# Hybrid decoder step on one core: weights of two experts asked for earlier, and gathered rows transposed by VectorE instead of TensorE

## The chip, the core and the metric

The kernel runs on one core of a Trainium2 chip. A core has five engines that run their own instruction streams and meet at semaphores: TensorE (PE, matrix products and transposes into PSUM), VectorE (DVE), ScalarE (ACT), GpSimd (POOL) and SyncE (SP). SP and POOL also ask for the transfers between HBM and SBUF, which 16 DMA engines carry out. The metric is the device time of one execution in microseconds; less is better.

## The reference, cut to what matters

One layer: a token mixer (mLSTM and retention heads, one input and one output projection) and then a mixture of experts. 512 prompt rows and 64 sample rows, 576 rows of 1024 values in float32. What the change touches is the mixture:

```
def moe(h, w_router, b_router, we_g, we_u, we_d, ws_g, ws_u, ws_d):
    s = sigmoid(h @ w_router)                       # 64 experts
    eidx = ...                                      # 8 experts for each row, from 4 of 8 groups
    wts = s at eidx, normalised, times 2.5
    for each block of 128 rows of one expert e (tok, wt):
        xb = h[tok]
        hb = silu(xb @ we_g[e]) * (xb @ we_u[e])    # 1024 -> 256
        acc[tok] += wt * (hb @ we_d[e])             # 256 -> 1024
    return acc + (silu(h @ ws_g) * (h @ ws_u)) @ ws_d
```

An expert has 2 MB of gate and up weights and 1 MB of down weights: 64 experts, some 200 MB, each read once.

## The kernel before

Every engine's program is written out by hand, and every wait in it is a semaphore wait that holds up all that stands behind it on that engine. The first part (about 450 us) is the mixer. Then come `y_mm` (the output projection, row tile by row tile), the second norm, the router and the shared expert's up products, and then the expert stage.

**Blocks.** The experts are sorted by how many rows chose them (the first three, `NPRE`, are experts 0, 1, 2, whatever their counts, so that their weights can be asked for before the ids are known). `CAPS` gives each a fixed number of 32-row pieces, 192 in all, so 48 blocks (`NBK`) of 4 pieces, numbered 0 to 47. A block can hold pieces of up to four experts.

**A block on each engine.** `place` (DVE, L2202 and L2205) builds a 0/1 matrix for the block three ahead, `find_idx` (PE, L1536) turns it into row numbers, `idx_out` (DVE, L2241 to L2243) stores them. POOL gathers the rows (`gather`, L790) into one of three buffers `xg`, three blocks ahead. `x_T` (PE, L1549) transposes the 128 x 1024 rows by eight 128 x 128 transposes into two PSUM banks, and ScalarE (`xT_evac`, L1053) and VectorE (`xT_evac`, L2247) copy half each into `xT`. `up` (PE, L1561) multiplies by the gate and up weights, in 8 chunks of the contraction. `silu` (ACT) and `gated` (DVE, L2255) follow, `hh_T` (PE, L1572) transposes the 256 columns, `down` (PE, L1584) multiplies by the down weights, two copies (`out_rows`, DVE L2262) bring the rows to `yo`, and POOL scatters them (`scatter`, L806).

The order on PE in block b is `up(b)`, `hh_T(b-1)`, `x_T(b+1)`, `find_idx(b+3)`, `down(b-1)`. In the last block, 47, `hh_T` stands between the first six chunks of `up` and the last two. The order on DVE is `place(b+3)`, `xT_evac(b+1)`, `gated(b)`, `idx_out(b+3)`, `out_rows(b-1)`.

**Weights.** Five slots (`WSLOTS`) hold the weights of five experts; the r-th expert in the sorted order uses slot r % 5. SP asks for the weights in a fixed order: the gate and up weights (`load_gate_up`, L616) of expert r once `up` of the last block of expert r-5 is done, the down weights (`load_dn`, L620) once its `down` is. One slot lies in `x_sb` and `hT`, where the residual rows and the router's input are until late. Two slots lie at the start of `mem`, where the mixer's output weights and temporaries are, one behind them, and one (`NM`) in a stretch that holds small tables and the last retention state. SP's order before the stage: `b_router`, the stores of the five tiles of `mixed_rows`, the shared expert's down weights, then (when the rows for the gathers are stored) experts 0 and 1, the gate and up weights of expert 2, and, when the sorted ids are there (`tab_ready`), the gate and up weights of experts 3 and 4; the down weights of experts 2, 3 and 4 come when the shared up products are done.

Of the kernel before, what the change touches and what calls it, by code (L numbers as in the profile page):

```python
# [14 lines left out]
P = 128  # L15
# [31 lines left out]
XSLOT = 2  # L47
XSLOT2 = 4
OVSLOTS = [0, 1, 3]
XG = 3  # L50
OVMAX = 4 * U
# [83 lines left out]
def build(nc, A, O, K):  # L135

    ctx = ExitStack()
    with ctx:
# [151 lines left out]
        def yT(h):  # L290
# [14 lines left out]
        W_AT = [0, WSZ, None, w2_at, NM]  # L305
# [4 lines left out]
        at = w2_at + WSZ  # L310
        hhT, at = carve(mem, at, [FJ * BLK])
# [9 lines left out]
        dn4, e_ = carve(mem, e_, [FJ, D])  # L321
        at = max(at + NT * D, e_)
# [47 lines left out]
            P_ready idx_mm idx_ready gat0 gat1 gat2 xgT_t xgT_a xgT_d eup egs ehh ehT_t ehT edn eout_a eout_d sct0 sct1  # L370
# [92 lines left out]
        def wview(r):  # L463

            if slot(r) == XSLOT:
                return x_flat[:, 0:2 * KC * FE].rearrange("p (c n) -> p c n", c=KC), dnX
            at_ = W_AT[slot(r)]
            gu = mem[:, at_:at_ + 2 * KC * FE].rearrange("p (c n) -> p c n", c=KC)
            if slot(r) == XSLOT2:
# [4 lines left out]
        GU_LOADED = [("ld_gu0", 0), ("ld_gu1", 0), ("ld_gu2", 0), ("ld_gu3", 0), ("ld_a1", 32)]  # L474
        DN_LOADED = [("ld_d0", 0), ("ld_d1", 0), ("ld_d2", 0), ("ld_d3", 0), ("ld_a2", 32)]
# [54 lines left out]
        def _(sp):  # L530
# [115 lines left out]
            sp.wait_ge(S["xgT_t"], NBK)  # L646
# [12 lines left out]
            def last_rows():  # L659
                sp.wait_ge(S["xgT_a"], nov + (NBK + 1))  # L660
                sp.wait_ge(S["xgT_d"], nov + (NBK + 1))
# [5 lines left out]
            sp.wait_ge(S["xgT_a"], NBK)  # L667
            sp.wait_ge(S["xgT_d"], NBK)
# [43 lines left out]
        def _(pool):  # L712
# [80 lines left out]
            def ahead(n, q, g):  # L793
                pool.wait_ge(S["idx_ready"], n + 1)
                if not isinstance(n, int):
                    pool.wait_ge(S["xgT_t"], n - 1)
# [48 lines left out]
        def _(act):  # L845
# [227 lines left out]
            def body(n, j, s, i):  # L1073
                silu(n, j)
                xT_evac(n + 1, j + 1)
# [18 lines left out]
            overflow(act, nov, body, lambda: xT_evac(NBK, NBK))  # L1094
# [16 lines left out]
        def _(pe):  # L1111
# [427 lines left out]
            def x_T(n, j, s=None):  # L1539

                g = gbuf(n, j)
                pe.wait_ge(S[f"gat{g}"], gcount(n, j, s))
                if not (isinstance(n, int) and n == 0):
                    pe.wait_ge(S["xgT_a"], n)
                    pe.wait_ge(S["xgT_d"], n)
# [6 lines left out]
            def up(n, j, parts, cs=range(KC)):  # L1552

                pe.wait_ge(S["xgT_a"], n + 1)
                pe.wait_ge(S["xgT_d"], n + 1)
# [42 lines left out]
            def body(n, j, s, i):  # L1598
# [3 lines left out]
                x_T(n + 1, j + 1, s + 1)  # L1602
# [14 lines left out]
            x_T(0, 0)  # L1617
# [27 lines left out]
            def first_blocks():  # L1645
                whole = [(slice(0, BLK), 0, None)]
                find_idx(NBK, NBK, whole)
                x_T(NBK, 0, 0)
                find_idx(NBK + 1, NBK + 1, whole)

            def last_done():
                pe.wait_ge(S["xgT_a"], nov + (NBK + 1))
                pe.wait_ge(S["xgT_d"], nov + (NBK + 1))
# [8 lines left out]
            for name in ("xgT_a", "xgT_d", "ehh", "ehT", "eout_a", "eout_d", "idx_ready"):  # L1662
                pe.wait_ge(S[name], NBK)

            def shared_down(o, js=range(FJ)):
                t, kp = COMBINE[o]
                n = ROWS[t]
                if o == 0:
                    pe.wait_ge(S["ld_br"], 32)
# [38 lines left out]
        def _(dve):  # L1708
# [370 lines left out]
            dve.wait_ge(S["ld_br"], 32)  # L2079
# [165 lines left out]
            def xT_evac(n, j):  # L2245
                dve.wait_ge(S["xgT_t"], n + 1)
                cp(xT[:, j % 2, 4 * BLK:8 * BLK], ps[1][:, :]).then_inc(S["xgT_d"], 1)  # L2247
# [16 lines left out]
            def body(n, j, s, i):  # L2264
                place_more(n + 2, j + 2, s + 2)
                gated(n, j)
                xT_evac(n + 1, j + 1)
# [31 lines left out]
            def first_blocks():  # L2299
# [3 lines left out]
                xT_evac(NBK, NBK)  # L2303
# [184 lines left out]
```

## Time and profile before

| | |
|---|---|
| median of 3 runs | 1125.05 us (1124.58 to 1125.45) |
| the profiled execution's own time | 1126.64 us |
| its span (first to last instruction) | 1124.8 us |
| TensorE busy | 1094.1 us, 97% of the span |
| VectorE busy | 462.7 us, 41% |
| ScalarE busy | 236.4 us, 21% |
| mean over the span that the DMA moved | 300 GB/s |

The profile lists each engine's instructions with start and duration, in microseconds from the start of the span, and the packets of the DMA. An "idle" time of an instruction is how long its engine stood still ahead of it, with the instruction or the transfer that ended the wait. "To landing" is the time from the issue of a transfer until its last piece is there. L numbers are lines of the kernel.

### The profile page before, as it was taken

Reading aid. Unit: us, or ns where it says so; the run is one execution under the profiler, and the core shown is the slowest. Engines: PE = TensorE matmul, PEld = TensorE weight load, DVE = VectorE, ACT = ScalarE, POOL = GpSimd, SP = SyncE. Lnnn points to the kernel's source line nnn. Section 1 sums busy time; section 2 is a strip of 40 time slices with the busy share of each in tenths; the row PEclk is TensorE's granted clock in tenths of the full one; section 3 lists DMA queues with packets and bytes.
Section 4 is the critical chain, followed back from the end, with each engine's and each line's share of the span. In section 5 each row is a group of like instructions: output and inputs, shape, how many; then the busy total and the mean of one; then the engine's idle time right before and its main releaser. Section 6 shows DMA issues by size and latency. Waiting matters only on the chain.

```text
span 1124.8 us, 16922 instructions
## 1 busy us (share of the span) xinstructions
PE 1094.1 (97%) x6443; PEld 575.1 (51%) x6443; DVE 462.7 (41%) x1286; ACT 236.4 (21%) x516; POOL 135.3 (12%) x163
## 2 busy tenths in 40 slices
PE   6999999999999999999999999999999999999896
PEld 3456677777877545754343443443444444343232
DVE  2218541565456645843274233233232232331157
ACT  4131241222133123211111111111111111111111
POOL 0210000000020010121112112111111121121100
PEclk9999999999999999999999999999999999999999
DMA  9857622021170273899999999999999999999598
GB/s 370 326 207 295 227 79 75 1 85 51 62 266 7 103 255 120 311 365 426 423 425 426 424 417 425 425 416 396 421 409 384 426 399 400 417 391 370 209 412 344
DMA packets 51655, 337.16 MB, mean 300 GB/s; under 512 B 9637, under 2 KB 14089, under 8 KB 30831
## 3 DMA queue, kind: packets, MB, share of 16 engines
q1 hardware_dynamic: 33710, 287.32, 63.0%
q0 software_dynamic: 17856, 48.68, 11.8%
q8 instruction: 54, 0.88, 0.3%
q14 instruction: 35, 0.28, 0.1%
HBM read 311.30 MB, written 37.24 MB: 310 GB/s over the span
## 4 chain that ended last, share of the span: by engine, by line
PE 91%; DMA 4%; DVE 2%; ACT 1%; issue 1%; SPq 0%; DVEq 0%; POOLq 0%; ACTq 0%
PE bank L1561 30%; PE bank L1584 15%; PE bank L1257 10%; PE bank L1276 5%; PE bank L1549 4%; DMA mem<-expert_out_rows 3%; PE bank L1375 3%; PE bank L1376 3%; PE bank L1170 3%; PE bank L1493 3%; PE bank L1254 3%; PE bank L1145 1%; PE bank L1572 1%; PE bank L1340 1%; PE bank L1154 1%; PE bank L1128 1%
## 5 line engine op out<-in xcount | busy, mean ns | idle before, releaser
L1561 PE MATMUL bank<-mem 128*32 128x512 f32 (+2 forms) x1488 | 304.5, 594 | 0.6 <-DVE mem L2247 0.6
L1561 PEld LDWEIGHTS bank<-mem 128*32 128x32 f32 (+2 forms) x1488 | 100.6, 126 | 166.0 <-issue 166.0
L1584 PE MATMUL bank<-mem 128*32 128x512 f32 (+2 forms) x744 | 157.0, 596 | 0.1
L2247 DVE COPY mem<-bank 128x512 f32<-128x512 f32 x48 | 33.2, 691 | 283.3 <-PE bank L1549 283.3
L1257 PE MATMUL bank<-hT,mem 128*128 128x288 f32 x512 | 133.3, 410 | 1.0 <-ACT mem L935 1.0
L1257 PEld LDWEIGHTS bank<-hT,mem 128*128 128x128 f32 x512 | 93.9, 190 | 25.7 <-issue 2.4
L1561 PE MATMUL bank<-x_sb,mem 128*32 128x512 f32 (+2 forms) x416 | 99.3, 594 | 0.0
L1065 ACT ACTIVATE mem<-bank 128x256 f32<-128x256 f32 x48 | 18.4, 384 | 313.0 <-PE bank L1572 312.8
L1584 PEld LDWEIGHTS bank<-mem 128*32 128x32 f32 (+2 forms) x744 | 48.7, 126 | 61.4 <-issue 60.6
L2262 DVE COPY hT<-bank 128x512 f32<-128x512 f32 x48 | 33.2, 691 | 85.7 <-PE bank L1584 85.6
L790 POOL DMA_INDIRECT mem<-ffn_in_rows,idxg x32 | 32.9, 1028 | 264.5 <-DVE idxs L2243 211.0
L806 POOL DMA_INDIRECT expert_out_rows<-hT,idxs x48 | 48.7, 1015 | 114.8 <-DVE hT L2262 110.4
L1071 ACT ACTIVATE hT<-bank 128x512 f32<-128x512 f32 x48 | 28.7, 597 | 140.8 <-PE bank L1584 140.8
L1561 PEld LDWEIGHTS bank<-x_sb,mem 128*32 128x32 f32 (+2 forms) x416 | 32.2, 127 | 49.4 <-issue 49.4
L1276 PE MATMUL bank<-mem 128*128 128x512 f32 x128 | 56.3, 594 | 0.0
L1584 PE MATMUL bank<-hT,mem 128*32 128x512 f32 (+2 forms) x208 | 51.0, 596 | 1.1 <-ACT mem L1065 1.1
L2205 DVE SCALAR_TENSOR_TENSOR mem<-mem,c_full 128x160 bf16<-128x160 f32 (+3 forms) x77 | 43.9, 570 | 0.3 <-issue 0.3
L1375 PE MATMUL bank<-hT,mem 128*128 128x288 f32 x128 | 42.4, 413 | 0.0
L1376 PE MATMUL bank<-hT,mem 128*128 128x288 f32 x128 | 41.5, 406 | 0.0
L1276 PEld LDWEIGHTS bank<-mem 128*128 128x128 f32 x128 | 23.8, 190 | 27.4 <-issue 27.2
L1053 ACT ACTIVATE mem<-bank 128x512 f32<-128x512 f32 x48 | 28.7, 597 | 38.8 <-PE bank L1549 38.8
L2255 DVE SCALAR_TENSOR_TENSOR mem<-mem,wtab,bank 128x128 f32<-128x128 f32 x96 | 29.1, 344 | 17.3 <-ACT mem L1059 17.3
(400 smaller groups left out, 1281.2 us busy)
## 6 DMA issues: line engine op xcount, KB each, us to landing
mem<-k_w_exp SPq DMA_DIRECT2D x51, 2048.0 KB, 23.3
mem<-in_w_exp_down SPq DMA_DIRECT2D x51, 1024.0 KB, 22.7
x_sb<-k_w_exp SPq DMA_DIRECT2D x13, 2048.0 KB, 21.4
mem<-k_w_ada SPq DMA_DIRECT2D x8, 2048.0 KB, 9.0
mem<-k_w_in SPq DMA_DIRECT2D x7, 2048.0 KB, 9.7
hT<-in_w_exp_down SPq DMA_DIRECT2D x13, 1024.0 KB, 25.4
mem<-expert_out_rows SPq DMA_DIRECT2D x6, 2048.0 KB, 16.5
mem<-k_w_head SPq DMA_DIRECT2D x4, 2048.0 KB, 18.4
```

What stands on the lines that cost most here:

```text
L806: pool.indirect_dma_start(y_d[:, :], bass.IndirectOffsetOnAxis(idxs[:, q:q + 1], 0), yo[:, q % 2, :], None, bounds_check=T * TOPK - 1, oob ...
L1170: i = mm(ps[t][:, :], hT[:, k, t * P:(t + 1) * P], ring[:, 0, k * 512:(k + 1) * 512], start=k == 0, stop=k == KC - 1)
L1254: i = mm(bank[0:n, 0:2 * DH], hT[:, k, c * P:c * P + n], w[:, k, 2 * DH * hf:2 * DH * (hf + 1)], start=k == 0, stop=k == KC - 1)
L1257: i = mm(bank[:, 0:TH], w[:, k, c * P:(c + 1) * P], hT[:, k, hf * TH:(hf + 1) * TH], start=k == 0, stop=k == KC - 1)
L1276: i = mm(y_half(t, hf), yT(k)[:, t * P:t * P + n], wo[:, k, hf * 512:(hf + 1) * 512], start=k == 0, stop=k == 2 * H - 1)
L1375: mm(A0[:, 0:TH], st, hT[:, k, 0:TH], start=k == 0, stop=k == KC - 1)
L1376: i = mm(A1[:, 0:TH], st, hT[:, k, TH:T], start=k == 0, stop=k == KC - 1)
L1493: i = mm(ps[bu if m else bg][:, 0:TH], gu_s[:, m, k, j * P:(j + 1) * P], hT[:, k, hf * TH:(hf + 1) * TH], start=k == 0, stop=k == KC - 1)
L1549: i = tr(ps[c // 4][:, (c % 4) * BLK:(c % 4 + 1) * BLK], xg[g][:, c * P:(c + 1) * P], ident[:, :])
L1561: i = mm(bank[sl, :], xT[:, j % 2, c * BLK + sl.start:c * BLK + sl.stop], wview(r)[0][:, c, :], start=c == 0, stop=c == KC - 1)
L1584: i = mm(ps[4 + hf][sl, :], hhT[:, k * BLK + sl.start:k * BLK + sl.stop], wview(r)[1][:, k, hf * 512:(hf + 1) * 512], start=k == 0, stop=k ...
L2205: return stt(pm, p.to_broadcast([P, NT, w]), off, iota[:, 0:w].unsqueeze(1).to_broadcast([P, NT, w]), ALU.add, ALU.is_equal)
```

## The change

Two edits.

1. The slots are numbered anew: the first is the one at `NM`, with its down weights where the mixer's gates were, then the two at the start of `mem`, the one behind them, and last the one in `x_sb` and `hT`. Expert 0 is asked for right behind `b_router`, expert 1 when `y_mm` is done (in front of the store of the fifth tile of `mixed_rows`), expert 2 with its down weights when the rows for the gathers are stored. The shared expert's down weights follow behind it, and `b_router` gets another semaphore.
2. For the blocks from number 10 on (`TURNED`), VectorE transposes the gathered rows from `xg` to `xT` by itself: `turn`, 16 instructions of 32 partitions x 256 values, each of eight 32 x 32 blocks. `x_T` and its two copies remain for blocks 0 to 9. From block 9 on, `hh_T` stands between the first six chunks of `up` and the last two. The semaphores `xgT_t` and `xgT_d` for the finished rows give way to `xT_ready`.

```
@@ constants @@
-XSLOT = 2
-XSLOT2 = 4
-OVSLOTS = [0, 1, 3]
+EXTSLOT = 0
+XSLOT = 4
+OVSLOTS = [1, 2, 3]
 XG = 3
+TURNED = 10
...
-        W_AT = [0, WSZ, None, w2_at, NM]
+        W_AT = [NM, 0, WSZ, w2_at, None]
...
+        at += gate_at - at
+        dn4, at = carve(mem, at, [FJ, D])
...
@@ SP @@
-            sp.dma_start(brow, A["b_router"][0].partition_broadcast(P)).then_inc(S["ld_br"], 16)
-            for t in range(NT):
-                sp.wait_ge(S["x1_done"], t + 1)
-                sp.dma_start(x1_d[t * P:t * P + ROWS[t], :], x_sb[0:ROWS[t], t, :]).then_inc(S["st_x"], 16)
-            load_down(sp, dn_s, A["w_sh_down"][0], S["ld_br"])
-            sp.wait_ge(S["h2T_t"], NT)
-            sp.wait_ge(S["h2_st0"], 16 * ((NT + 1) // 2))
-            sp.wait_ge(S["h2_st1"], 16 * (NT // 2))
+            sp.dma_start(brow, A["b_router"][0].partition_broadcast(P)).then_inc(S["ld_col"], 16)
...
-            for r in range(2):
-                load_gate_up(r, r)
-                load_dn(r, r)
+            load_gate_up(0, 0)
+            load_dn(0, 0)
+            for t in range(NT):
+                if t == NCH:
+                    sp.wait_ge(S["y_mm"], NT)
+                    load_gate_up(1, 1)
+                    load_dn(1, 1)
+                sp.wait_ge(S["x1_done"], t + 1)
+                sp.dma_start(x1_d[t * P:t * P + ROWS[t], :], x_sb[0:ROWS[t], t, :]).then_inc(S["st_x"], 16)
+            sp.wait_ge(S["h2T_t"], NT)
+            sp.wait_ge(S["h2_st0"], 16 * ((NT + 1) // 2))
+            sp.wait_ge(S["h2_st1"], 16 * (NT // 2))
+            load_gate_up(2, 2)
+            load_dn(2, 2)
+            load_down(sp, dn_s, A["w_sh_down"][0], S["ld_br"])
             sp.wait_ge(S["st_x"], 16 * NT)
-            load_gate_up(XSLOT, XSLOT)
             sp.wait_ge(S["tab_ready"], 1)
...
             load_gate_up(NPRE, id3)
-            load_gate_up(NPRE + 1, id4)
+            load_gate_up(XSLOT, id4)
             sp.wait_ge(S["gu_mm"], NSH)
-            load_dn(XSLOT, XSLOT)
             load_dn(NPRE, id3)
-            load_dn(NPRE + 1, id4)
+            load_dn(XSLOT, id4)
...
             sp.wait_ge(S["eup"], max(LASTB[r] for r in range(NE) if slot(r) == XSLOT) + 1)
-            sp.wait_ge(S["xgT_t"], NBK)
+            sp.wait_ge(S["xT_ready"], NBK)
...
@@ POOL, ahead() @@
                 elif n >= XG:
-                    pool.wait_ge(S["xgT_t"], n - XG + 1)
+                    pool.wait_ge(S["xT_ready"], n - XG + 1)
...
@@ ACT @@
-                if b < NBK - 1:
+                if b + 1 < TURNED:
                     xT_evac(b + 1, b + 1)
...
@@ PE @@
             for b in range(NBK):
                 new_gu(b)
-                if b < NBK - 1:
-                    up(b, b, pieces(b))
-                else:
-                    up(b, b, pieces(b), range(KC - 2))
+                split = KC if b + 1 < TURNED else KC - 2
+                up(b, b, pieces(b), range(split))
...
                     hh_T(b - 1)
-                if b == NBK - 1:
-                    up(b, b, pieces(b), range(KC - 2, KC))
-                if b < NBK - 1:
-                    x_T(b + 1, b + 1)
+                if split < KC:
+                    up(b, b, pieces(b), range(split, KC))
+                if b + 1 < TURNED:
+                    x_T(b + 1)
...
@@ DVE @@
+            def turn(n, j, s=None):
+
+                g = gbuf(n, j)
+                dve.wait_ge(S[f"gat{g}"], gcount(n, j, s))
+                dve.wait_ge(S["eup"], n - 1)
+                rows = xg[g].rearrange("s (c d) -> s c d", c=KC)
+                cols = xT[:, j % 2, :].rearrange("d (c s) -> d c s", c=KC)
+                for q in range(P // QS):
+                    for a in range(P // QS):
+                        sl, dl = slice(q * QS, (q + 1) * QS), slice(a * QS, (a + 1) * QS)
+                        i = dve.transpose(cols[dl, :, sl], rows[sl, :, dl])
+                i.then_inc(S["xT_ready"], 1)
...
-                if b < NBK - 1:
+                if b + 1 < TURNED:
                     xT_evac(b + 1, b + 1)
+                elif b + 1 < NBK:
+                    turn(b + 1, b + 1)
                 gated(b, b)
```

## Rows read from the trace of the kernel before

**Rows 1.** The page: busy time of the engines, and the DMA in 40 slices.
```profile
PE 1094.1 (97%) x6443; PEld 575.1 (51%) x6443; DVE 462.7 (41%) x1286; ACT 236.4 (21%) x516; POOL 135.3 (12%) x163
...
DMA  9857622021170273899999999999999999999598
```

**Rows 2.** Waits of TensorE, 485 to 1058 us: total, times, longest.
```profile
PE bank L1584 <- ACT mem L1065: 1.1, 1, 1.1
PE bank L1561 <- DVE mem L2247: 0.6, 1, 0.6
```

**Rows 3.** TensorE in order of time, block 20 and the start of 21.
```profile
723.34 7.13 PE L1561 MATMUL bank<-x_sb,mem 128*128 128x512 f32 x16
730.31 0.38 PE L1572 MATMUL bank<-c_ident,mem 128*128 128x128 f32 x2
730.53 1.04 PE L1549 MATMUL bank<-c_ident,mem 128*128 128x128 f32 x8
731.49 0.29 PE L1536 MATMUL bank<-mem 128*32 128x7 bf16 x20
731.75 3.67 PE L1584 MATMUL bank<-mem 128*128 128x512 f32 x8
735.35 1.06 PE L1561 MATMUL bank<-mem 128*32 128x512 f32 x8
```

**Rows 4.** Stretches: busy PE, PEld, DVE, ACT, POOL; clock, DMA share, GB/s.
```profile
485.00:765.00 280.00, 279.18 (x2080) 117.87 (x2082) 100.94 (x267) 42.64 (x92) 47.24 (x47) 1.00 1.01 420
765.00:1045.00 280.00, 280.00 (x1783) 116.23 (x1775) 79.72 (x227) 43.87 (x95) 45.29 (x45) 1.00 0.98 399
1010.00:1020.00 10.00, 10.00 (x57) 4.28 (x54) 3.22 (x11) 1.37 (x4) 1.00 (x1) 1.00 0.76 291
```

**Rows 5.** Gate/up loads (L616) issued 706 to 708 us: issue, landing.
```profile
L616 SPq DMA_DIRECT2D mem<-k_w_exp x2: 333/333/333, 706.7 to 707.8; - x2
...
DMA to landing us min/median/max: 28.0/30.4/32.9
```

**Rows 6.** The same, issued 1028 to 1030 us.
```profile
L616 SPq DMA_DIRECT2D mem<-k_w_exp x1: 333/333/333, 1028.8 to 1028.8; - x1
...
DMA to landing us min/median/max: 15.0/15.0/15.0
```

**Rows 7.** TensorE in order of time, block 47: start of `up`, start of `down`.
```profile
1045.06 0.64 PE L1561 MATMUL bank<-x_sb,mem 128*64 128x512 f32 x1
...
1052.50 1.89 PE L1584 MATMUL bank<-mem 128*64 128x512 f32 x8
```

**Rows 8.** Gate/up load issued 1004 to 1006 us: issue, landing.
```profile
L616 SPq DMA_DIRECT2D mem<-k_w_exp x1: 333/333/333, 1004.7 to 1004.7; - x1
...
DMA to landing us min/median/max: 18.5/18.5/18.5
```

**Rows 9.** SP's queue in order of time, 395 to 520 us.
```profile
460.07 0.33 SPq L616 DMA_DIRECT2D mem<-k_w_exp  x1
...
485.14 0.89 SPq L616 DMA_DIRECT2D mem<-k_w_exp  x2
487.25 0.34 SPq L620 DMA_DIRECT2D hT<-in_w_exp_down  x1
```

**Rows 10.** VectorE's groups by shape, 600 to 1000 us: busy us, mean ns.
```profile
L2247 DVE COPY mem<-bank 128x512 f32<-128x512 f32 x34 | 23.5, 691 | 209.3 <-PE bank L1549 209.3
...
L2205 DVE SCALAR_TENSOR_TENSOR mem<-mem,c_full 128x480 bf16<-128x480 f32 x16 | 10.4, 653 | 0.0
...
L2205 DVE SCALAR_TENSOR_TENSOR mem<-mem,c_full 128x160 bf16<-128x160 f32 x16 | 5.1, 321 | 0.0
```

**Rows 11.** The gathers (L790), all 48.
```profile
DMA to landing us min/median/max: 4.6/10.6/12.3
```

**Rows 12.** Stretches behind the last block, columns as in rows 4.
```profile
1061.00:1064.00 3.00, 0.20 (x2) 0.00 (x0) 0.69 (x1) 0.60 (x1) 0.96 (x1) 1.00 0.30 93
1064.00:1068.00 4.00, 3.92 (x6) 1.16 (x7) 0.22 (x1) 0.00 (x0) 0.00 (x0) 0.57 0.24 79
```

More of the change, by code:

```diff
@@ L320, in build @@
         bcG, e_ = carve(mem, e_, [2, D])
-        dn4, e_ = carve(mem, e_, [FJ, D])
-        at = max(at + NT * D, e_)
+        at = e_
         R, at = carve(mem, at, [8, NT, NE], dt=BF16)
@@ L468, in wview @@
             gu = mem[:, at_:at_ + 2 * KC * FE].rearrange("p (c n) -> p c n", c=KC)
-            if slot(r) == XSLOT2:
+            if slot(r) == EXTSLOT:
                 return gu, dn4
@@ L472, in wview @@
             return gu, dn
-        GU_LOADED = [("ld_gu0", 0), ("ld_gu1", 0), ("ld_gu2", 0), ("ld_gu3", 0), ("ld_a1", 32)]
-        DN_LOADED = [("ld_d0", 0), ("ld_d1", 0), ("ld_d2", 0), ("ld_d3", 0), ("ld_a2", 32)]
+        GU_LOADED = [("ld_a1", 32), ("ld_gu0", 0), ("ld_gu1", 0), ("ld_gu2", 0), ("ld_gu3", 0)]
+        DN_LOADED = [("ld_a2", 32), ("ld_d0", 0), ("ld_d1", 0), ("ld_d2", 0), ("ld_d3", 0)]
         def gu_sem(r):
@@ L659, in last_rows @@
             def last_rows():
-                sp.wait_ge(S["xgT_a"], nov + (NBK + 1))
-                sp.wait_ge(S["xgT_d"], nov + (NBK + 1))
+                sp.wait_ge(S["xT_ready"], nov + (NBK + 1))
                 sp.wait_ge(S["sct0"], 16 * (NBK // 2) + 16 * ((nov + 1) // 2))
@@ L666, in _ @@
             overflow(sp, nov, body, last=last_rows)
-            sp.wait_ge(S["xgT_a"], NBK)
-            sp.wait_ge(S["xgT_d"], NBK)
+            sp.wait_ge(S["xT_ready"], NBK)
             for k in range(2):
@@ L795, in ahead @@
                 if not isinstance(n, int):
-                    pool.wait_ge(S["xgT_t"], n - 1)
+                    pool.wait_ge(S["xT_ready"], n - 1)
                 elif n >= XG:
-                    pool.wait_ge(S["xgT_t"], n - XG + 1)
+                    pool.wait_ge(S["xT_ready"], n - XG + 1)
                 pool.sem_inc(S["pool_step"], 1)
@@ L1093, in _ @@
             out_rows(NBK - 1, NBK - 1)
-            overflow(act, nov, body, lambda: xT_evac(NBK, NBK))
+            overflow(act, nov, body)
             for i, (t, _) in enumerate(COMBINE):
@@ L1537, in find_idx, with x_T @@
                 i.then_inc(S["idx_mm"], 1)
[L1539 to L1543, printed above, removed]
+            def x_T(n):
+                g = gbuf(n, n)
+                pe.wait_ge(S[f"gat{g}"], gcount(n, n))
+                if n:
                     pe.wait_ge(S["xgT_a"], n)
-                    pe.wait_ge(S["xgT_d"], n)
+                    pe.wait_ge(S["xT_ready"], n)
                 else:
@@ L1552, in up @@
             def up(n, j, parts, cs=range(KC)):
-                pe.wait_ge(S["xgT_a"], n + 1)
-                pe.wait_ge(S["xgT_d"], n + 1)
+                if isinstance(n, int) and n < TURNED:
+                    pe.wait_ge(S["xgT_a"], n + 1)
+                pe.wait_ge(S["xT_ready"], n + 1)
                 if not (isinstance(n, int) and n < 2):
@@ L1601, in body @@
                 up(n, j, whole)
-                x_T(n + 1, j + 1, s + 1)
                 find_idx(n + 2, j + 2, whole)
@@ L1616, in _ @@
             shared_up(KC // 2)
-            x_T(0, 0)
+            x_T(0)
             shared_up(2)
@@ L1647, in first_blocks @@
                 find_idx(NBK, NBK, whole)
-                x_T(NBK, 0, 0)
                 find_idx(NBK + 1, NBK + 1, whole)
             def last_done():
-                pe.wait_ge(S["xgT_a"], nov + (NBK + 1))
-                pe.wait_ge(S["xgT_d"], nov + (NBK + 1))
+                pe.wait_ge(S["xT_ready"], nov + (NBK + 1))
                 pe.wait_ge(S["ehh"], nov + NBK)
@@ L1661, in _ @@
             overflow(pe, nov, body, first_blocks, last_done)
-            for name in ("xgT_a", "xgT_d", "ehh", "ehT", "eout_a", "eout_d", "idx_ready"):
+            for name in ("xT_ready", "ehh", "ehT", "eout_a", "eout_d", "idx_ready"):
                 pe.wait_ge(S[name], NBK)
@@ L1668, in shared_down @@
                 if o == 0:
-                    pe.wait_ge(S["ld_br"], 32)
+                    pe.wait_ge(S["ld_br"], 16)
                     pe.wait_ge(S["sh_ready"], NSH)
@@ L2077, in _ @@
                     bcB[0:n, 1, :].rearrange("p (q c) -> p q c", c=KC), ALU.add).then_inc(S["h2_ready"], 1)
-            dve.wait_ge(S["ld_br"], 32)
+            dve.wait_ge(S["ld_col"], 32)
             dve.memset(gs12, -MARK)
@@ L2246, in xT_evac @@
                 dve.wait_ge(S["xgT_t"], n + 1)
[L2247 removed]
+                cp(xT[:, j % 2, 4 * BLK:8 * BLK], ps[1][:, :]).then_inc(S["xT_ready"], 1)
+            def turn(n, j, s=None):
[9 more added lines that the diff above has]
+                i.then_inc(S["xT_ready"], 1)
             def gated(n, j):
@@ L2266, in body @@
                 gated(n, j)
-                xT_evac(n + 1, j + 1)
+                turn(n + 1, j + 1, s + 1)
                 idx_out(n + 2, j + 2, s + 2)
@@ L2302, in first_blocks @@
                 place_more(NBK + 1, NBK + 1, 1)
-                xT_evac(NBK, NBK)
+                turn(NBK, 0, 0)
                 idx_out(NBK + 1, NBK + 1)
```

3 lines of the change are left out of this document (1 added, 2 removed).

## The prediction

> **What bounds the kernel now.** I read the page first, then the waits of TensorE, then one block of the expert stage in order of time, then the DMA side of that stage. The page shows TensorE busy for 1094.1 of 1124.8 us and, from the eighteenth of its 40 slices on, the DMA engines at 9 tenths almost throughout [rows 1]. Two things are full at once, so the question is which of them would give way. From 485 to 1058 us TensorE waited twice, 1.7 us in all [rows 2]. It is the engine that sets the pace. A block takes 12.0 us: from the start of `up` of one block at 723.34 to the start of the next at 735.35 [rows 3]. The eight transposes of the gathered rows (`x_T`, L1549) start at 730.53, and the work behind them at 731.49: 0.96 us of the block.
>
> Now the transfers. Over the first 280 us of the stage the engines moved 420 GB/s at a mean share of 1.01, over the next 280 us 399 GB/s at 0.98 [rows 4]. A 2 MB gate/up load would need 5 us at 420 GB/s. The pair issued at 706.7 and 707.8 took 28.0 and 32.9 us [rows 5]: each stands behind several others, and the queue of loads is never empty there. Next, how early a load is. By the list of capacities the load issued at 706.7 is that of the thirtieth expert, which block 21 needs first, and block 21 starts at 735.35 [rows 3]. It lands at 706.7 + 28.0 = 734.7. That is 0.65 us before use. The last load of all is issued at 1028.8, lands 15.0 us later at 1043.8 [rows 6], and block 47 starts at 1045.06 [rows 7]: 1.26 us early. So loads are just in time twice, at the middle and at the very end, with the queue full. TensorE sets the pace, with the DMA about one microsecond behind it.
>
> One more row says how hard this second limit is. The load issued at 1004.7 took 18.5 us and landed at 1023.2 [rows 8], yet from 1010 to 1020 us the mean share of the 16 engines was 0.76 [rows 4]. Some engines had run dry while others still held pieces of a load that nobody could use before the last piece. The mean share understates how busy the last engine is.
>
> **The change part by part.** *Transposes off TensorE.* For blocks 10 to 47 the eight transposes go, 38 times. The order inside these blocks becomes six chunks of `up`, `hh_T`, two chunks of `up`, `find_idx`, `down`. Block 47 has this order already, without `find_idx`: from the start of `up` to the start of `down` it takes 1052.50 - 1045.06 = 7.44 us [rows 7]. An ordinary block takes 731.75 - 723.34 = 8.41 us, of which `find_idx` holds 0.26 us [rows 3]. TensorE saves 8.41 - 7.44 - 0.26 = 0.71 us a block, 27.0 us in all, if it waits for nothing else.
>
> *What the transfers let through.* Nothing of the 64 loads, gathers and scatters goes away. A load is still issued when a block frees its slot; issued earlier, it stands longer in the same queue. The time at which the last gate/up load lands moves only by what is taken off the queue ahead of it.
>
> *The early loads.* Before, experts 0, 1 and 2 are asked for from 460.07 on, and what needs the sorted ids follows at 485.14; the third expert's down weights wait until 487.25, in the midst of the full stretch [rows 9]. After, expert 0 is asked for right behind `b_router`, before the first row store, expert 1 in front of the last store of `mixed_rows`, and expert 2 takes their old place together with its down weights. For experts 0 and 1 this gains nothing by itself: they were in time already. What gets out of the queue behind 485 is that one 1 MB transfer: 1.05 MB / 420 GB/s = 2.5 us. Experts 3 and 4 still wait for the ids. The cost of the early loads: the fifth store of `mixed_rows` stands behind 3 MB, 7.5 us at 420 GB/s, and with it the clearing of the third gather buffer. Cover is the stretch from 460.07 to 485.14 [rows 9], so I take nothing; without the cover it would be 7.5 us. `w_sh_down` moves behind expert 2, and is now wanted only after the last block. The read back of `mixed_rows` into `x_sb` waits for block 45 instead of 47, since the slot there is now another one: it stands behind the last weights on SP's queue, so no load waits for it, and its 2.36 MB, 5.6 us at 420 GB/s, are through before the last scatter.
>
> *VectorE.* Per block it drops one copy of 0.69 us and gets 16 transposes of 32 x 256 values. The trace has no transpose on VectorE. The fixed part and the slope come from two forms of the same line: 160 columns take 0.321 us, 480 take 0.653 [rows 10], so 1.04 ns a column and 0.155 us fixed, 0.42 us for 256. Bounds: 0.32 (the 160-column form) and 0.69 (the copy of 512 columns). I take 0.42, since these forms go column by column, and a transpose moves each value once, too: 16 x 0.42 = 6.7 us. VectorE was busy 79.72 us of 280 [rows 4], 3.4 us of a block of 12.0. Afterwards: 3.4 - 0.69 + 6.7 = 9.4 us. That fits into a block, and TensorE waits for none of it. On VectorE the `gated` product and the index row stand behind the turn; both are wanted in the next block, `gated` only after six chunks of `up`. The gather, asked for at the end of a block's chain, landed after 12.3 us at worst [rows 11]; the turn that needs it comes two blocks later, so it is in time by a few tenths or more. ScalarE loses a copy, and nothing waited 1 us or more for that one [rows 2].
>
> The Trainium skill speaks against this part: in "VectorE: DVE Perf Modes", section "The three transpose paths", VectorE does 32 x 32 blocks only, and the rules for authors send a full 128 x 128 transpose to TensorE. Its 311 ns for 128 x 128 values of bf16 would make an estimated 2.5 us for eight, instead of my 6.7; the time that I forecast is the same by either, as both are covered.
>
> *The sum.* After the early blocks TensorE runs ahead of the loads and waits for them. Block 47 can start when the last gate/up load lands: 1043.8 - 2.5 = 1041.3 instead of 1045.06, so 3.7 us. A cost comes back: where TensorE stood still for 2.8 of 3 us, the clock granted in the next 4 us was 0.57, a mean of the full 2.4 GHz and the lower level of 1.2 GHz [rows 12]. If a wait ahead of block 47 does that, it costs 4 x (1 - 0.57) = 1.7 us. Bounds 0 and 1.7; I take 0.7, since most such waits fall where the loads are late anyway. 3.7 - 0.7 = 3.0 us. What follows block 47 is unchanged. The profiled execution took 1126.64 us for a span of 1124.8, and the median is 1125.05, so taking 3.0 us from the median gives 1122.0 us.
>
> **The rivals.** *A, the idle share of the DMA is usable.* If 399 GB/s in the second half were no limit but only a lack of requests, earlier requests would fill it: 280 x (1 - 399/420) = 14 us more, 1108 us. For it: the 0.76 between 1010 and 1020. Against it: a load was outstanding all that time. The Trainium skill, "DMA: Bandwidth & Descriptors", section "iDMA fabric", has it that a bulk load runs at the pace of its slowest engine; by that A is out, and the trace agrees with its 18.5 us beside a share of 0.76.
>
> *B, the loads are hidden anyway.* Then all 27.0 us come off: 1098 us. Against it: 0.65 us at block 21, and 1.26 us at block 47.
>
> *C, slower: VectorE becomes the bound.* The place is the turn, in front of `gated` on one engine. The point is (12.0 - 2.7) / 16 = 0.58 us for a transpose. At 0.69 us, the row of the 512-column copy, a block takes 2.7 + 11.0 = 13.7 us, 1.7 us more, 38 times: 1125 + 65 = 1190 us. At 0.60 it is 1136 us. For it: no transpose has been seen. Against it: 256 columns are half of that copy's.
>
> *D, nothing changes.* The queue is so full that the 2.5 us and the last 1.3 us are lost to scatters which, with TensorE ahead, come in front of the last loads, and to the clock: between 1123.5 and 1127 us.
>
> **How the numbers follow.** About 0.2%, 2.25 us, is what a measurement of this kernel can tell from no change. My forecast, 1119 to 1123.5 us, gets 0.55; A, with what lies between it and the forecast, 0.15; B 0.03; C, or another late step of VectorE, 0.12; D 0.15. The likeliest case gives 1122.0. For 8 in 10 the range reaches to A, 1108, and up through D to the mildest form of C, 1130. Faster: most of the forecast (0.41 of 0.55, since its upper end is at the limit), A and B: 0.59. Same: the rest of the forecast and most of D: 0.26. Slower: C and a little of D: 0.15.
>
> **What would show it.** L1549 stands in the profile 80 times instead of 384. TensorE, which waited 1.7 us, waits some 20 to 27 us for the weights in the blocks from about the eighteenth on, and the blocks without a wait take 11.2 to 11.3 us. The shares of the DMA rise a little, and the last gate/up load lands at about 1041 us, not some 15 us earlier. VectorE's transposes take about 0.42 us and its busy share rises to 0.8 of a block. I am wrong if TensorE waits little and the span falls by over 8 us (then the DMA had room), or if TensorE waits for VectorE instead of the loads (then C).

## The result, and the profile after

The changed kernel takes 1128.67 us (median of 6 runs, 1127.59 to 1130.65), the kernel before 1125.25 us beside it: a ratio of 1.0029, 95% interval 1.0018 to 1.004. It is slower by 0.3%. The forecast was 1122.0 us and faster; the time lies inside the range of 1108 to 1130.

The profiled execution took 1129.68 us, 3.04 us more than the one of before. The page, the lines that answer to [rows 1], and VectorE's transposes:

```profile
PE 1070.1 (95%) x6139; PEld 541.8 (48%) x6139; DVE 698.8 (62%) x1856; ACT 218.1 (19%) x478; POOL 135.5 (12%) x163
...
PEclk9999999999999999999999999999999899899999
DMA  9857622022170386699999999999999999999598
...
L2257 DVE STREAM_TRANSPOSE mem<-mem 32x256 f32<-32x256 f32 x400 | 174.2, 435 | 5.3
...
L2257 DVE STREAM_TRANSPOSE mem<-x_sb 32x256 f32<-32x256 f32 x208 | 90.6, 436 | 2.7
```

TensorE works 24 us less, a transpose takes 0.436 us, and VectorE has 570 instructions more. The waits of TensorE from 485 to 1070 us (total, times, longest), to be read against [rows 2], and the stretches with the columns of [rows 4]:

```profile
PE bank L1564 <- issue: 23.1, 8, 6.0
PE bank L1587 <- DMA mem<-in_w_exp_down: 1.9, 1, 1.9
...
PE bank L1564 <- DMA mem<-k_w_exp: 0.7, 1, 0.7
```

```profile
485.00:765.00 280.00, 270.48 (x1974) 106.62 (x1976) 192.79 (x490) 36.21 (x79) 47.03 (x46) 0.99 1.01 418
765.00:1045.00 280.00, 265.16 (x1581) 93.78 (x1573) 224.01 (x576) 32.39 (x71) 45.21 (x45) 0.98 0.98 397
...
1048.00:1052.00 4.00, 4.00 (x14) 1.42 (x12) 0.00 (x0) 0.00 (x0) 0.00 (x0) 0.57 0.98 368
```

TensorE's 24 us come back as 25.7 us in which it stands still for weights. Most of it is put down to "issue", that is, to nothing that the profile names. `up` waits for several semaphores at once; at block 47 the wait ends 0.1 us behind the last part of the load (1047.14 and 1047.23 us), and I read the others in the same way. The DMA moves no more than before. Block 47, TensorE in order of time, against [rows 7], and the last gate/up load, against [rows 6]:

```profile
1047.23 7.07 PE L1564 MATMUL bank<-mem 128*64 128x512 f32 x24 [3.07 <-issue]
1054.22 0.44 PE L1575 MATMUL bank<-c_ident,mem 128*128 128x128 f32 x2
```

```profile
L611 SPq DMA_DIRECT2D mem<-k_w_exp x1: 332/332/332, 1027.5 to 1027.5; - x1
...
DMA to landing us min/median/max: 19.6/19.6/19.6
```

For the sum at the end, where the first six chunks of block 47 end in the kernel before, and the last scatter before and after:

```profile
1050.36 0.44 PE L1572 MATMUL bank<-c_ident,mem 128*128 128x128 f32 x2
...
1062.78 4.95 DMA expert_out_rows<-hT,idxs
```

```profile
1066.64 3.23 DMA expert_out_rows<-hT,idxs
```

The load is asked for 1.3 us earlier than before and lands 3.3 us later, at 1047.1 instead of 1043.9. Block 47 waits for it and starts 2.17 us later. Its first six chunks take 6.99 us (1047.23 to 1054.22); before, they took 5.30 (1045.06 to 1050.36). In the changed kernel TensorE had stood still for 3.07 us, and the granted clock from 1048 to 1052 us is 0.57. That makes 3.9 us. The chain of waits behind it gives 0.8 us back. The last scatter takes 1.7 us less (3.23 us, not 4.95; the read back of `x_sb` is now asked for at 1044.79 instead of 1052.71, but no run shows that this is the reason), and the last read of the experts' rows takes 1.4 us more. At the end 3.1 us are left.

### The profile page after: what moved, and what is told of

It reads as the page before. It is cut to its first block, busy times and chain, and to the rows that moved or that the text cites. A ratio compares the mean times of both kernels' runs of the same rounds, so it can differ in the third digit from the quotient of the medians.

```text
span 1127.9 us, 16862 instructions
## 1 busy us (share of the span) xinstructions
PE 1070.1 (95%) x6139; PEld 541.8 (48%) x6139; DVE 698.8 (62%) x1856; ACT 218.1 (19%) x478; POOL 135.5 (12%) x163
## 4 chain that ended last, share of the span: by engine, by line
PE 84%; DMA 10%; issue 2%; DVE 2%; ACT 1%; SPq 0%; DVEq 0%; POOLq 0%; ACTq 0%
PE bank L1564 27%; PE bank L1587 14%; PE bank L1259 10%; PE bank L1278 5%; DMA mem<-expert_out_rows 3%; DMA mem<-in_w_exp_down 3%; PE bank L1377 3%; PE bank L1378 3%; PE bank L1495 3%; PE bank L1172 3%; PE bank L1256 3%; DMA mem<-k_w_exp 2%; PE bank L1147 1%; PE bank L1575 1%; PE bank L1342 1%
## 5 line engine op out<-in xcount | busy, mean ns | idle before, releaser
L1564 PE MATMUL bank<-mem 128*32 128x512 f32 (+2 forms) x1504 | 331.9, 607 | 24.4 <-issue 23.1
L1564 PEld LDWEIGHTS bank<-mem 128*32 128x32 f32 (+2 forms) x1504 | 106.6, 129 | 206.6 <-issue 205.0
L2257 DVE STREAM_TRANSPOSE mem<-mem 32x256 f32<-32x256 f32 x400 | 174.2, 435 | 5.3
L1587 PE MATMUL bank<-mem 128*32 128x512 f32 (+2 forms) x752 | 166.1, 604 | 1.1 <-ACT mem L1068 1.1
L1564 PE MATMUL bank<-x_sb,mem 128*32 128x512 f32 (+2 forms) x400 | 109.9, 607 | 0.0
L2257 DVE STREAM_TRANSPOSE mem<-x_sb 32x256 f32<-32x256 f32 x208 | 90.6, 436 | 2.7
L1587 PEld LDWEIGHTS bank<-mem 128*32 128x32 f32 (+2 forms) x752 | 52.4, 128 | 72.2 <-issue 71.4
L1587 PE MATMUL bank<-hT,mem 128*32 128x512 f32 (+2 forms) x200 | 56.4, 605 | 1.9 <-DMA mem<-in_w_exp_down 1.9
```

The lines of the kernel that those rows point to most:

```text
L1564: i = mm(bank[sl, :], xT[:, j % 2, c * BLK + sl.start:c * BLK + sl.stop], wview(r)[0][:, c, :], start=c == 0, stop=c == KC - 1)
L1587: i = mm(ps[4 + hf][sl, :], hhT[:, k * BLK + sl.start:k * BLK + sl.stop], wview(r)[1][:, k, hf * 512:(hf + 1) * 512], start=k == 0, stop=k ...
L2257: i = dve.transpose(cols[dl, :, sl], rows[sl, :, dl])
```

## The experiments

All numbers are medians of 4 to 11 runs; the kernel before had 1125.0 to 1126.1 us beside them. "Parts": the trace has the 16 times at which each load raises its semaphore. There are 16 DMA engines, and I read each time as the landing of one engine's share; the trace doesn't say which engine's. Sorted, in us from the start of the span, for the last gate/up load of the kernels that matter:

```
                              asked for  1st     8th     12th    15th    16th part (us)
before                        1028.8   1036.7  1037.3  1038.2  1043.7  1043.9
changed                       1027.5   1036.0  1036.8  1037.4  1042.0  1047.1
one transpose (e3)            1021.2   1029.9  1030.5  1036.3  1041.9  1042.1
early loads alone (e1)        1028.1   1036.1  1036.6  1037.3  1040.2  1040.9
early loads, dummy work (e16) 1027.8   1037.2  1037.6  1038.8  1041.2  1044.8
both transpose (e4)           1034.9   1043.1  1043.7  1044.1  1044.4  1047.2
before, dealt by eights (e9)  1033.0   1041.2  1042.7  1050.2  1053.7  1053.9
before, even (e13)            1028.5   1036.6  1037.0  1037.2  1037.3  1038.4
changed, even (e10)           1011.0   1019.9  1021.6  1022.9  1024.0  1030.8
even, one transpose (e14)     1008.3   1017.7  1023.3  1024.4  1025.0  1027.1
even, 16 small (e17)          1013.3   1022.2  1022.6  1023.4  1025.3  1031.8
even, one large (e18)         1008.1   1017.1  1023.5  1024.2  1025.1  1026.8
even, reversed (e19)          1019.1   1027.8  1028.9  1034.1  1037.0  1037.3
```

### Which half does it, and by way of which engine

e1, the early loads alone, is `TURNED = 48`. e2, the turn alone, has the old slots and the old order on SP. In e3 the loop of `turn` is one instruction, `dve.transpose(cols[0:QS, :, 0:QS], rows[0:QS, :, 0:QS])`. e4 adds this where `x_T` stood:

```
+                elif b + 1 < NBK:
+                    for c in range(KC):
+                        tr(ps[c // 4][:, (c % 4) * BLK:(c % 4 + 1) * BLK], ident[:, :], ident[:, :])
```

> The early loads and the new slots alone: TensorE transposes the gathered rows of all 48 blocks, VectorE turns none. Theory 1 (VectorE's 16 transposes a block slow the transfers of the slowest DMA engine) and theory 2 (TensorE running ahead harms itself: earlier scatters in front of the last loads, half clock behind each wait) both expect 1122 to 1125.3 us: loads land some 2.5 us earlier than before at block 21, TensorE waits for none, and the read back of x_sb, asked for two blocks earlier, may give up to 2 us at the end. Theory 3 (the early loads themselves do the harm) expects over 1126 us.

> The turn by VectorE from block 10 on alone: slots, their semaphores and SyncE's order of loads as before. Theories 1 and 2 expect the changed kernel's time and the 2.5 us that the early loads took off the queue: 1130 to 1132 us, with more waits of TensorE for weights from about block 18 on. Theory 3 expects less than the changed kernel, under 1127 us.

> The changed kernel with 1 of the 16 transposes in each turn, so that most of the columns that up reads are not the gathered rows; TensorE's order is that of the changed kernel. Theory 1 (VectorE's traffic slows the transfers) expects the last gate/up load at about 1041.5 us and a time of 1121 to 1124 us. Theory 2 (TensorE ahead of the loads) expects the time of the changed kernel, 1127.5 to 1130 us, and the same windows of half clock.

> The changed kernel, and TensorE does eight transposes of a constant in each block from the tenth on, where x_T stood, into banks that nobody reads: TensorE keeps the pace of before, VectorE does all of its transposes. Theory 1 expects loads as late as in the changed kernel, with waits of TensorE of some us near the end, 1126 to 1129 us. Theory 2 expects no waits, no half clock, and 1122 to 1125.3 us as for the early loads alone.

Measured: e1 1125.18 us (ratio 0.9994, 0.9985 to 1.0003), e2 1131.23 (1.004, 1.0027 to 1.0053), e3 1122.02 (0.9962, 0.9948 to 0.9975), e4 1132.41 (1.0055, 1.0041 to 1.0068). The early loads do no harm, and no good while TensorE sets the pace, so theory 3 falls. The 2.5 us that were counted for them fit the landings of the last load, which is 2.1 us earlier with the turn (1047.1 us, in e2 1049.3) and 2.9 us earlier without it (1040.9, before 1043.9). In the times they are not shown clearly: the medians of e2 and the changed kernel are 2.6 us apart, their ratios only 1.2 us, and the intervals of the ratios overlap. In e3 TensorE runs ahead and waits much as in the changed kernel, and the time is the forecast's. Its waits for the loads, and its block 47:

```profile
PE bank L1564 <- issue: 17.7, 7, 4.7
...
1042.23 5.37 PE L1564 MATMUL bank<-mem 128*64 128x512 f32 x24 [0.72 <-issue]
```

So theory 2 falls: what costs 6.7 us is VectorE's 15 further transposes. e4 missed both expectations: the dummy transposes took 1.07 us a block, block 47 started at 1051.26 us, TensorE waited for no weight, and its own longer blocks set the time. Its parts tell something all the same: 15 of them land within 1.3 us, and the last one 2.8 us behind those, though TensorE doesn't run ahead. Such a late part comes with the turn, then, and not with TensorE's pace.

### Traffic, waiting, or something else

e5 has, in place of 15 transposes, 13 copies of 32 x 256 values within PSUM, each waiting for the one before. In e6 each `dve.transpose(a, b)` of the turn is a plain copy. The turn of e11 has its first 13 transposes where the turn stood, and the last 3 behind the index row:

```
                 elif b + 1 < NBK:
-                    turn(b + 1, b + 1)
+                    turn(b + 1, b + 1, part=range(13))
                 gated(b, b)
                 if b + XG < NBK:
                     idx_out(b + XG, b + XG)
+                if TURNED <= b + 1 < NBK:
+                    turn(b + 1, b + 1, part=range(13, 16))
```

> The changed kernel with 1 of the 16 transposes in each turn and, ahead of it, 13 copies one after the other of 32 x 256 values from one PSUM bank into another: VectorE is held about as long as by 16 transposes (so the index row and the next gather are asked for as late), but SBUF is hardly read or written for it. Theory 1a (VectorE's traffic in SBUF slows the transfers) expects the time with one transpose, 1121 to 1124 us. Theory 1b (the turn holds VectorE, and what stands behind it is asked for later) expects that of the changed kernel, 1127.5 to 1130 us.

> The changed kernel with each of the 16 transposes replaced by a copy of the same 32 x 256 values between the same places, so that nothing is transposed inside a 32 x 32 square. If any traffic of VectorE between these places slows the transfers, the time stays at 1127 to 1130 us; if only the transposing instruction does it, 1121 to 1124 us as with one transpose.

> The changed kernel, all 16 transposes kept, but only 13 of them stand ahead of gated and the index row and 3 behind: the next gather is asked for some 1.4 us earlier in a block, as early as with one transpose. Theory 1b (what stands behind the turn on VectorE is late) expects the time with one transpose, 1121 to 1124 us. If the time that VectorE reads and writes is what counts (theory 1a), or the last 3 transposes make up late, it stays at 1127 to 1130 us.

Measured: e5 1126.93 us (1.0019, 1.0009 to 1.0028), e6 1128.05 (1.0025, 1.0015 to 1.0035), e11 1127.81 (1.0021, 1.0012 to 1.003). Copies cost what transposes cost. e5 lies between its two expectations: 13 copies that leave SBUF alone cost three quarters of it, so it isn't mainly traffic in SBUF. With the index row in front, the time hardly moves, so it isn't what stands behind the turn either. At this point both explanations on offer had fallen.

### How the rows lie on the DMA engines

The gathers and scatters move 4 KB for each row that is there; an expert's rows fill its pieces from the top, so some partitions have more rows than others. e8 (on the changed kernel) and e9 (on the one before) deal the rows of a segment out in another order, by a table in place of `iota` in the comparison of `place`:

```
-    off, iota[:, 0:w].unsqueeze(1).to_broadcast([P, NT, w]),
+    off, spots[w].unsqueeze(1).to_broadcast([P, NT, w]),
...
+    spread = [np.arange(q * QS) % 8 * (q * QS // 8) + np.arange(q * QS) // 8 for q in range(1, 5)]
```

> The changed kernel with the rows of a block dealt out over the partitions: inside a segment of w slots, slot p stands at partition 8 x (p mod w/8) + p div (w/8) instead of p, through a table that the comparison in the block's placing reads in place of iota. With eight partitions to a DMA engine, the engine with the most gathered and scattered rows has 298 instead of 376 over the 48 blocks; 78 rows of 4 KB twice, at 0.17 us for 4 KB by the rate of that queue in the profile, are 27 us less on that engine. If the last of 16 uneven engines is what bounds the changed kernel, TensorE hardly waits any more and its 27 us come through: 1099 to 1106 us. If the bound is what all engines move together, the bytes are the same and so is the time: 1126 to 1130 us.

> The kernel before with the same dealing out and nothing else. TensorE set its pace and waited 1.7 us in the stage, so loads that land some 25 us earlier should give nothing: 1123.5 to 1127 us by every theory. If it were faster by over 5 us, TensorE would have been held up by something that its rows don't show.

Measured: e8 1133.41 us (1.0077, 1.0063 to 1.009), e9 1134.94 (1.0087, 1.0068 to 1.0107). Both went the wrong way, and the parts say why: in e9 eight land by 1042.7 and the rest from 1044.2 up to 1053.9. I had taken eight neighbouring partitions for one engine's. If they are four neighbouring ones, this dealing out puts about 370 rows on each of eight engines and about 200 on the others (counted from the routing of the inputs), which fits eight early and eight late parts. e10 and e13 deal by fours (8 in the table becomes 4), and e12 is e10 with the order of e11.

> The changed kernel with another dealing out of a segment's rows: slot p stands at partition 4 x (p mod w/4) + p div (w/4). The dealing out before this one left eight of the 16 parts of a load early and eight late, as it must if an engine serves four neighbouring partitions of each half (engine = partition div 4, mod 16) and not eight neighbouring ones: then it had put 366 to 375 rows on each of eight engines and about 200 on the others. By that the fullest engine has 360 rows in the changed kernel and 303 with this dealing out, 57 rows of 4 KB twice at 0.16 us each: 18 us less on the engine that lands last. Theory of the fullest engine: TensorE's waits fall by 13 to 18 us, 1110 to 1117 us. If not the fullest engine but all of them together are the limit, 1126 to 1130 us.

> The kernel before with the four-partition dealing out alone. TensorE sets its pace and waited 1.7 us in the stage, so earlier loads give nothing: 1123.5 to 1126.5 us, with the last gate/up load landing 10 us or more earlier than its 1044.

> Both of these together: four-partition dealing out, and 13 transposes ahead of the index row and 3 behind. If both theories hold the gains add up as far as TensorE still waits: 1104 to 1113 us. If only the fullest engine matters, as without the new order, 1110 to 1117 us.

Measured: e10 1112.87 us (0.9892, 0.9877 to 0.9907), e13 1125.14 (0.9997, 0.9988 to 1.0007), e12 1112.48 (0.9884, 0.9869 to 0.99). In e13 the last load lands within 1.8 us from first to last part and 5 us earlier than before, not the 10 us that I expected; TensorE, which sets the pace, can't use it. In e10 TensorE can. The same bytes move, the fullest engine has fewer of them by that count, and 16 us come off the changed kernel, as expected before the run. e12 adds nothing clear to it. TensorE's waits for `up`, in the changed kernel 23.1 us, here in e10:

```profile
PE bank L1565 <- issue: 11.9, 6, 4.1
```

The Trainium skill, "DMA: Bandwidth & Descriptors", section "The descriptor swizzle", puts four partitions and the four that lie 32 further on one engine (0 to 3 with 32 to 35) in a plain transfer of 128 partitions, where my expectation had those that lie 64 further. By the Trainium skill's map, taken over to gathers and scatters, an estimate from the routing of the inputs has the fullest engine go from 369 to 310 rows, by mine from 360 to 303. Both give the eight and eight of e9; no run here tells them apart.

### One late part: number or work

In e10 15 of the 16 parts land within 4.1 us, and the last one alone 6.8 us behind. With one transpose and the same rows it is 2.1 us behind (e14, below), so the rows alone don't make it late. The distance builds up over the stage: in e10 it is 0.1 us for the load asked for at 610.7 us, 3.9 for that at 795.2 and 6.8 for the last, in e14 0.9 for the loads asked for at 610.7 and 793.9. I read this as one engine that is slowed. e7 has 8 of the 16 transposes (`for a in range(P // QS // 2)`), e14 is e10 with the one transpose of e3. e16 is e1 with 14 idle transposes in each block, one after the other, from a constant into a spare place. e17 is e10 with each transpose cut to a 32 x 32 square; e18 is e10 with one instruction for all.

```
@@ e16 @@
+                for k in range(14 if 9 <= b < NBK - 1 else 0):
+                    step(dve.transpose(here, there))
@@ e17 @@
-                        i = dve.transpose(cols[dl, :, sl], rows[sl, :, dl])
+                        i = dve.transpose(cols[dl, 0, sl], rows[sl, 0, dl])
@@ e18, in place of the loop @@
+                i = dve.transpose(xT[:, j % 2, :], xg[g])
```

> The changed kernel with 8 of the 16 transposes in each turn (the other columns are not the gathered rows). If the loss grows with VectorE's work, the time lies half way between one transpose and sixteen: 1124 to 1127 us. If it sets in only where VectorE's chain of a block gets long, it stays near 1122 us.

> The changed kernel with the even dealing out and 1 of the 16 transposes in each turn (most columns are not the gathered rows). If VectorE's work slows every transfer, the 6.7 us between 16 transposes and 1 are there again: 1105 to 1108 us. If it did harm only by way of the uneven engines, the time is that with all transposes and even rows, 1111 to 1114 us.

> The early loads alone (TensorE transposes all gathered rows, at the pace of before), and VectorE does 14 more transposes of 32 x 256 constants one after the other in each block from the tenth on, into a place that nobody reads, where the turn stood. If VectorE's work slows the transfers, the loads land some 5 us later than with the early loads alone, the last gate/up load at about 1046 instead of 1041 us, TensorE waits, and the time rises to 1126 to 1131 us. If it does not, loads land as in that run and the time stays at 1124 to 1126 us.

> The changed kernel with even rows, each of the 16 transposes cut to one 32 x 32 square of eight (the other columns are not the gathered rows): the number of instructions of all transposes, an eighth of the work. If the number counts (one DMA engine fetches VectorE's code beside its rows), 1111 to 1114 us as with whole transposes, and one part of each load far behind the other 15. If the work counts, 1106.5 to 1109 us as with one transpose.

> The changed kernel with even rows and one transposing instruction of 128 x 1024 values in each turn, which turns every 32 x 32 square in its own four partitions' group (so the columns are not in their places): all the bytes that 16 transposes read and write, in one instruction. If the number counts, 1106.5 to 1109 us as with one small transpose; if the bytes count, 1111 to 1114 us.

Measured: e7 1124.63 us (0.9988, 0.9979 to 0.9997), e14 1107.37 (0.9839, 0.9825 to 0.9852), e16 1125.44 (0.9995, 0.9986 to 1.0004), e17 1113.4 (0.9886, 0.9871 to 0.99), e18 1107.9 (0.9842, 0.983 to 0.9855).

- The loss grows with the number: 1, 8 and 16 instructions a turn give 1122.02, 1124.63 and 1128.67 us.
- It is as large with even rows: 1107.37 with one, 1112.87 with sixteen.
- e16 shows it beside TensorE's old pace. Its last load is asked for as in e1 and its 15th part lands 1.0 us later, but the 16th lands 3.8 us later. TensorE's pace covers that, so the time stays, and my expectation for a slowing missed there.
- e17 and e18 decide. Sixteen instructions with an eighth of the work cost all of it, and one instruction with all of the bytes costs next to nothing. The time for which VectorE is held isn't what counts either: the sixteen of e17 take 0.202 us each, less than half of the 0.436 us of whole ones, and cost as much.

The large instruction of e18, then the page of e18 and that of e17, VectorE's line and the second of the two queues that fetch instructions (packets, MB):

```profile
L2255 DVE STREAM_TRANSPOSE mem<-mem x25: 1232/1237/1241, 596.6 to 1001.0; 128x1024 f32<-128x1024 f32 x25
```

```profile
PE 1065.3 (96%) x6139; PEld 542.1 (49%) x6139; DVE 481.1 (44%) x1286; ACT 217.7 (20%) x478; POOL 134.7 (12%) x163
...
q14 instruction: 32, 0.26, 0.1%
```

```profile
PE 1068.5 (96%) x6139; PEld 543.1 (49%) x6139; DVE 557.1 (50%) x1856; ACT 218.0 (20%) x478; POOL 135.1 (12%) x163
...
q14 instruction: 37, 0.30, 0.1%
```

That queue counts 32 packets in e3 and e14, 34 in e7, 36 in e5, and 37 in the changed kernel, e6, e10 and e11. Over the whole span it doesn't go by VectorE's instructions alone: the kernel before has 35 and e1 32, with 1286 instructions each. In the stage from 485 to 1045 us it does: 15 packets in the kernel before, e1 and e3, 17 in e7, 19 in e5 and e16, and 20 in the changed kernel.

### Away from the late engine

e19 is e10 with the dealing out the other way round: `q * QS - 1 -` ahead of the table's terms, which then gives the first engines the fewest rows.

> The changed kernel, whole, with the even dealing out the other way round: slot p of a segment stands where slot w - 1 - p stood. The first DMA engines get the fewest rows (258, 263, 264 and 270 on engines 0 to 3 instead of 303, 301, 294 and 286), the last the most (308, 311 and 314 on engines 13 to 15 instead of 285, 282 and 279). In the kernels with uneven rows the late part under much VectorE work was behind even the engines with 360 rows, so the slowed engine should be one of engines 0 to 3; with some 25 to 45 rows fewer it has 8 to 14 us less to do, and the 5 us of its fetching are covered: 1105 to 1110 us. If the slowed engine is one of the last, it gets some 30 rows more: 1117 to 1122 us.

Measured: 1117.49 us (0.9933, 0.9913 to 0.9953). The number falls into the second case, but its reason doesn't: the single late part is gone, 0.3 us behind the 15th instead of 6.8. Instead five parts are 6 us and more behind the first. By the count of rows these should be the engines that got more, and e19 takes 4.6 us longer than e10. That no single part is late any more fits a slowed engine among those that lost rows, or one that is hidden behind the fullest; which one it is stays open.

## Why the prediction was wrong, step by step

**What bounds it.** Right: TensorE's pace with the transfers close behind, and of those the engine that lands last. e10 and e13 show the second half of it.

**Transposes off TensorE.** Right, and a little low. A block without a wait takes 11.1 us (`up` starts at 805.27 and 816.38), so 0.9 us less than before, where 0.71 had been worked out.

**The early loads.** Right in the landings, where 2.1 and 2.9 us stand for the 2.5, and they help only beside the turn; in the times the size is not settled.

**VectorE.** The duration was right (0.42 against 0.436 us), and TensorE indeed never waits for a turn. This is the step that failed: "That fits into a block, and TensorE waits for none of it." The cost of the turn was looked for in VectorE's time and in what waits for it, and put at nothing. The 570 further instructions have a cost that no row of VectorE shows: the last part of each load falls behind, at the very place where the forecast had already found the bound. It is 6.7 us (1128.67 - 1122.02), 5.0 us by which block 47 starts later than in e3, and 1.7 us of the lower clock. Without it the sum comes out: e3 takes 1122.02 us where 1122.0 was predicted, its last gate/up load lands at 1042.1 us and block 47 starts at 1042.23. That it comes out to the tenth is partly luck. Block 47 starts 2.8 us earlier than before, where 3.7 were summed; the 0.7 us taken off for the clock didn't come; and 1.3 us are gained behind block 47, which the sum took as unchanged.

**What the transfers let through.** "The time at which the last gate/up load lands moves only by what is taken off the queue ahead of it" left out that something could be added, or slowed, on one engine alone.

**The clock.** The mechanism was right; the term was 0.7, and in the profiled execution block 47 paid 1.7, the upper bound. In e3 the first six chunks of block 47 took 5.30 us again (1042.23 to 1047.53), with TensorE idle for only 0.72 us ahead of them.

**The rivals.** A was wrong as put, since earlier requests alone filled nothing: the second half still moved 397 GB/s. Rows dealt out evenly filled some of it: 408 GB/s in e10. What was weighed against A, that a load waits for its last part, is what decided the case: e10 has the same bytes and takes 15.8 us less. (The Trainium skill, "DMA: Bandwidth & Descriptors", section "iDMA fabric", says that a bulk load runs at the pace of its slowest engine, inside an explanation that it calls unconfirmed; e10's 15.8 us agree.) B is out by the waits of 25.7 us. C is out: its place was right, the turn, but not its price nor its way. D came nearest, and its reasons, lost microseconds at the end and the clock, are part of it; the measured time lies above D's 1127 us, and D's scatters in front of the last loads are not what did it, since in e3 TensorE runs ahead too and no time is lost.

**What stays open.** That the number of VectorE's instructions makes the last part late is shown by e17 and e18. That one engine is slowed is read from the parts. That the fetching of instructions does it is argued from the packet counts; something else that goes once for each instruction, such as the record that each leaves in this profile, is not excluded by any run. In the trace such a packet of 8 KB takes 0.31 us; five more are 1.6 us, not the 4.7 us by which the last part is further behind in e10 than in e14, nor the 5.5 us between their times. Nor is it the sum of what is fetched: the change takes 304 matmuls and their weight loads off TensorE, the first queue goes from 54 to 51 packets, and both queues together from 1.16 to 1.14 MB. Where the rest goes, no run here shows.

## What to carry to other kernels

When transfers are the bound, ask which of the 16 parts of a load lands last and what is behind it. Where a gathered row stands among the partitions was worth 16 us here, with the same bytes, and the runs fit four neighbouring partitions to an engine. Count the instructions that a change adds on VectorE, too, and not only their durations; no run here tries another engine. Many small ones slowed the transfers here though they fit in idle time, so one large instruction that does the same work is worth a look. The version to keep is the changed kernel with even rows (1112.5 to 1112.9 us, 1.1% faster than the kernel before).

## What the runs showed of the hardware

- Fourteen instructions of VectorE more in each of 38 blocks made the last part of a load land 3.8 us later, while the others that the table lists moved by 0.9 to 1.5 us (e16 against e1). In e10 the last part is 6.8 us behind the 15th, in e14 2.1 us.
- The Trainium skill, "Runtime: NRT & Kernel Launch", section "Instruction fetch mechanics", calls the cost of crossing from one fetched block of code to the next mostly hidden. If that covered the transfers too, e17 would take no longer than e18; it takes 5.5 us longer, and the measurement decides. No run shows the fetching itself hold a transfer up.
- One transposing instruction of 128 x 1024 float32 values took 1.237 us; sixteen of 32 x 256, which together read and write the same values, took 16 x 0.436 = 7.0 us. With each in its own 32 x 32 square only, the large one doesn't replace the sixteen, but it sets the price of the smallness.
- A mean DMA share of 1.01 and 0.98 over 280 us each, in the changed kernel and in e10 alike, doesn't show that the last part is 5.1 and 6.8 us behind the 15th. The landing of the last part does.
